# Moving the loads of the second expert matrices of teams two to seven from SyncE's DMA queue to ScalarE's

## What is computed

```python
a = jnp.einsum('nd,edf->nef', hf, w1)
b = jnp.einsum('nd,edf->nef', hf, w3)
y = jnp.einsum('nef,efd->nd', jax.nn.silu(a) * b * comb[..., None].astype(h.dtype), w2)
```

## Time and profile before

| | |
|---|---|
| median of 3 runs | 1349.12 us (1348.98 to 1349.36) |
| the profiled execution's own time | 1352.52 us |
| its span | 1350.7 us |
| mean granted clock of TensorE | 0.859 |
| busy share of the span: TensorE, VectorE, ScalarE | 73%, 24%, 23% |
| moved by DMA | 480.66 MB, mean 356 GB/s over the span |

### The profile page before, as it was taken

How to read it: one execution, slowest core, us unless ns; L and a number is a source line. 1 busy time by engine, 2 the same in 40 slices (tenths; PEclk the granted TensorE clock), 3 DMA queues, 4 the chain that set the end, 5 groups by cost and what they waited for, 6 DMA issues and landing times.

```text
span 1350.7 us, 18973 instructions
## 1 busy us (share of the span) xinstructions
PE 989.4 (73%) x8270; PEld 656.2 (49%) x8270; DVE 330.6 (24%) x504; ACT 307.1 (23%) x553; POOL 71.7 (5%) x48
## 2 busy tenths in 40 slices
PE   7999999999999974656576375647736664674647
PEld 6988887888888651333134133313413421341322
DVE  5557967544753200010010000001001000100101
ACT  6545555555542410001001000100100010010000
POOL 0000242500010020000000000000000000000000
PEclk9999999999999987678787777878868776886778
DMA  8745645544697999999999999999999999999997
GB/s 285 242 140 168 206 150 196 182 162 153 181 419 265 395 428 437 431 427 436 431 433 429 439 432 427 437 434 430 429 438 433 427 437 435 427 431 436 432 423 292
DMA packets 65458, 480.66 MB, mean 356 GB/s; under 512 B 7272, under 2 KB 11776, under 8 KB 48512
## 3 DMA queue, kind: packets, MB, share of 16 engines
q1 hardware_dynamic: 65408, 479.95, 86.7%
HBM read 477.84 MB, written 2.10 MB: 355 GB/s over the span
## 4 chain that ended last, share of the span: by engine, by line
DMA 48%; PE 47%; SPq 2%; DVE 1%; issue 1%; ACT 1%; DVEq 0%; ACTq 0%
DMA ring<-w_dram 47%; PE ps L1587 11%; PE ps L1330 9%; PE ps L1331 9%; PE ps L1332 9%; PE ps L1625 5%; SPq L487 1%; DVE w_split L879 1%; PE ps L1346 1%; DMA xs<-x_dram 1%; SPq L400 1%; PE ps L1542 1%; PE ps L1440 1%; PE ps L1362 0%; SPq L407 0%
## 5 line engine op out<-in xcount | busy, mean ns | idle before, releaser
L1587 PE MATMUL ps<-ring,side_buf 128*32 128x256 f32 x3968 | 273.4, 443 | 240.0 <-DMA ring<-w_dram 240.0
L1587 PEld LDWEIGHTS ps<-ring,side_buf 128*32 128x32 f32 x3968 | 155.7, 127 | 362.3 <-issue 309.2
L1330 PE MATMUL ps<-w_split,zT_half 128*128 128x512 f32 (+2 forms) x576 | 221.8, 385 | 1.8 <-DVE w_split L879 1.7
L1332 PE MATMUL ps<-w_split,zT_half 128*128 128x512 f32 (+2 forms) x576 | 218.6, 379 | 0.0
L1331 PE MATMUL ps<-w_split,zT_half 128*128 128x512 f32 (+2 forms) x576 | 218.5, 379 | 0.0
L879 DVE TENSOR_TENSOR w_split<-raw_buf,w_split 128x1024 fp32r<-128x1024 f32 (+2 forms) x144 | 182.0, 1282 | 147.2 <-ACT w_split L597 146.6
L1625 PE MATMUL ps<-ring,side_buf 128*32 128x512 f32 x960 | 129.4, 700 | 98.9 <-DMA ring<-w_dram 98.0
L597 ACT CAST w_split<-raw_buf 128x1024 fp32r<-128x1024 f32 (+2 forms) x144 | 143.5, 1016 | 113.9 <-PE ps L1332 108.9
L1256 DVE TENSOR_TENSOR xs<-xs,ps 128x512 f32<-128x512 f32 x56 | 38.5, 687 | 487.8 <-PE ps L1554 487.7
L817 ACT ACTIVATE side_buf<-ps,st 128x256 f32<-128x256 f32 x16 | 6.7, 471 | 545.2 <-PE ps L1587 545.2
L1625 PEld LDWEIGHTS ps<-ring,side_buf 128*32 128x32 f32 x960 | 38.0, 126 | 184.9 <-issue 184.9
(11 more groups left out here) (186 smaller groups left out, 493.2 us busy)
## 6 DMA issues: line engine op xcount, KB each, us to landing
ring<-w_dram SPq DMA_DIRECT2D x56, 4096.0 KB, 24.7
ring<-w_dram SPq DMA_DIRECT2D x72, 2048.0 KB, 21.3
raw_buf<-w_in_dram SPq DMA_DIRECT2D x47, 1024.0 KB, 5.0
raw_buf<-w_out_dram SPq DMA_DIRECT2D x16, 1024.0 KB, 5.8
spare<-w_dram SPq DMA_DIRECT2D x2, 2048.0 KB, 8.7
ring<-w_dram SPq DMA_DIRECT2D x4, 1024.0 KB, 12.1
ring<-w_dram SPq DMA_DIRECT2D x8, 512.0 KB, 11.4
raw_buf<-w_in_dram SPq DMA_DIRECT2D x4, 608.0 KB, 6.1
```

The costliest lines, as they stand in the source:

```text
L1330: mm(b, zhi(c)[:, t], wh, start=(c == 0), stop=False)
L1332: last = mm(b, zlo(c)[:, t], wh, start=False, stop=(c == C - 1))
L1587: last = mm(ps[part, up, pair * WIDE:(pair + 1) * WIDE], h_e[:, c, slots], w[m][:, cc * NB + h * WIDE:cc * NB + (h + 1) * WIDE], start=(c ...
```

## The change

SP's loop over teams one to six issues only the U groups. ScalarE's program issues D0 and D1 of these teams, on its own DMA queue, with the same waits on `ring_used`, the same sources, slots and semaphores. Each team's D0 loads stand ahead of the two silus, D1's behind them. Team 0 is taken out of ScalarE's loop, since SP loads it, and so is the last team.

```diff
             with sp.Fori(1, TEAMS - 1) as it:
-                team(it, it)
+                matrices(it, it)
...
-            def team(it):
+            def load_down(it, half):
+
+                for m in range(TEAM):
+                    k = UP_CHUNKS + TEAM * half + m
+                    act.wait_ge(ring_used, it * TEAM_CHUNKS + (k - RING + 1))
+                    act.dma_start(ring[:, chunk_slot(k), :],
+                                  w2_v[bass.ds(it * TEAM + m, 1), half].rearrange("o p n -> (o p) n")).then_inc(
+                                      landed[chunk_slot(k)], 16)
+
+            def team(it, loads=False):
+                if loads:
+                    load_down(it, 0)
                 activate(it)
+                if loads:
+                    load_down(it, 1)
                 gathered(it + 1)
                 turned(it)
                 act.wait_ge(ring_used, it * TEAM_CHUNKS + TEAM_CHUNKS)
...
-            with act.Fori(0, TEAMS - 1) as it:
-                team(it)
+            team(0)
+            with act.Fori(1, TEAMS - 1) as it:
+                team(it, loads=True)
```

## The result

The changed kernel takes 1371.12 us (median of 5 runs, 1364.86 to 1373.75), the one before 1349.36 in runs beside it: a ratio of 1.0156, 95% interval 1.0143 to 1.0169, 21.8 us slower. Forecast was no change. The measured time lies inside the stated range, near the number of rival A, but A is not what happened.

A forecast was written before the change was run, and what follows sets the result against it. The prediction took the kernel's expert stage as bound by DMA bytes at one steady rate. Moved issues, ScalarE's delays and queue sharing each cost 0 for six teams, leaving the median unchanged at 1349.1 us; range 1347 to 1374.

The forecast's parts named there:

- rival A: Queues share equal bytes: U3 lands late, stream empty before D1's rows, 3.95 us lost a team; 1372.8 us, chance 0.15.
- The bound: Expert stage, 573 to 1310 us: bytes divided by one steady rate, DMA share 1.00 at 432 GB/s, 116.4 us a team.
- Turns by row, two to one: Queues share by rows: U's are 32.7 KB, D's 16 KB, so U gets two thirds of the rate, D one third.
- U3 against D0: D0 competes with the landing U3, which lands at 840.15, 5.3 us late; margin at D1's issue 1.35 us, cost 0.
- D1 against the next U0: D1, 3.5 us left, gets one third beside U0, lands 6.9 us late; margin at next U1 1.15 us, cost 0.
- The start of a transfer: Time from a DMA's issue to its first rows: 1.5 us, with 0 and 2.5 also tried for D1's margin.
- ScalarE's delay of the gather: D1's four issues on ScalarE hold up the gather's first copies; gather, turns and D0's matmuls 1.2 us later, cost 0.
- The team that I took: The one team clocked before the change, U2's matmuls ending at 822.70, from which both margins were worked out.
- theory 1: Not in the prediction, made for the follow-up runs: turns by row, 3.4 us from issue to first row beside a busy queue.
- B: Small holes close the margins of about 1 us: 0.5 to 1.3 us a team, 1352 to 1357 us, chance 0.15.
- How long an issue takes on ScalarE: ScalarE's DMA issue time, shown by no row; at twice SP's time the delay would be 3.5 us, still inside.
- the prediction's estimate from its fastest group: Limit on any gain: every group at the fastest pace, 19.30 us, saves 0.55 us a team, 3.3 in six; 1345.8 at best.

The follow-up runs named there:

- experiment 3: Changed kernel plus three or six useless TensorE matmuls a team between the turns and D0's matmuls: 1353.13 us (1.0045) and 1352.4 us (1.0027).
- cut_rows: Changed kernel with each 4 MB load of U issued as two DMAs of 2 MB in 16 KB rows: 1360.21 us, 1.0088 to the kernel before.
- d0_on_act: Changed kernel with D1 given back to SP, only D0 on ScalarE's queue: 1350.6 us, 1.0005 to the kernel before.
- pad3: Changed kernel plus three useless TensorE matmuls between the turns and D0's matmuls of each team but the last: 1353.13 us, 1.0045 to the kernel before.
- act_warm: Changed kernel with one 8 KB load moved from SP's to ScalarE's queue at the start: 1367.51 us, 1.0130 to the kernel before.

## Why the prediction was wrong

**The bound: right.** The expert stage is bytes at one rate; in experiment 3 TensorE got more work and the time went down.

**Turns by row, two to one: right**, by the counts of rows (35 and 34) and by `cut_rows`. Two queues brought no bandwidth either, `d0_on_act` standing at 1.0005. The traces agree with the Trainium skill's rule that the prediction named ("DMA: Bandwidth & Descriptors", Rules for kernel authors): 431 GB/s there from 573 to 1310 us, and 432 before. The same page of the Trainium skill (Queues, rings and completion order) has an engine drain a whole packet, typically 9 to 17 descriptors, before it turns to the next queue. Here 16 engines moved 16 rows of one queue and then 16 of the other, one row a turn, and the measurement decides. Rival A's share of equal bytes does not occur with these rows. Its 1372.8 us is near the measured time by accident: the hole stands behind D1, not before it.

**U3 against D0: right in kind.** "lands at 840.15, 5.3 us late" was 3.4 in the team shown, and 4.2 where U2's matmuls take 7.11 us as in the earlier trace rows. A start 3.4 us after the issue, not 1.5, leaves U3 more time alone.

**D1 against the next U0: the step that failed.** The text had "The stream holds until 893.05: margin 1.15 us"; by the losses it was minus 1.5 to minus 3.8 in teams two to six, and minus 9.2 in team one. From U2's landing to D1's I had 65.2 us (815.45 to 880.65); it took 68.0 in the team shown (825.67 to 893.64) and 66.7 in one where U2's matmuls take 7.11 us (944.64 to 1011.37). And U1 landed 2.6 us later than its issue and 19.4 us of stream (903.30 to 925.32), where I had put 1.5; in the other teams it was 2.8 to 3.6. Term by term:

- *The start of a transfer.* "I put at 1.5 us", at most 2.5. It is 3.4 to 3.5 beside a busy queue. The bound came from the shortest landing in a trace in which no second queue ever came up beside a first.
- *ScalarE's delay of the gather.* "1.2 us later": D0's matmuls started 10.0 us after U3's (858.51 to 868.51), against 9.85 before, 0.15. Nor did D1's first issue wait for the silus: it began at 739.69, the second silu at 739.85. I counted both as costs that eat a margin. They would have protected the other one: `pad3` gives such a delay back.
- *The team that I took.* U2's matmuls take 7.11 us there, in other teams 8.80. The longer ones issue D0 later, so U3 is less late, so U0 is asked for sooner, with D1 4.6 and not 3.5 us from done; at a third of the rate each of these is paid three times.

With 3.4 us for every start and 0.15 us for the gather, the prediction's own sum gives a hole of about 0.9 us in a team where U2's matmuls take 7.11 us, and with U2's end 1.7 us later about 2.6 us. Recorded are 1.5 and 2.2 for the first kind, 2.5, 2.6 and 3.8 for the second. So these terms make most of the loss of teams two to six; up to 1.3 us a team stays open.

**The error behind these** is that I checked each margin for lateness alone. With two queues, being early does harm: by theory 1, one us less before the next U0 lets D1's rest grow by one and its landing by two. A margin of 1.15 us with a gear of two or three on terms known to 1 us is not "0"; the chance of 0.15 for B, small holes of 0.5 to 1.3 us, was too low and their size too small. B's kind of thing is what happened.

**Team one, 9.2 us: missed.** "How long an issue takes on ScalarE no row shows; at twice SP's time the delay would be 3.5 us" was right for 44 issues (344 ns) and wrong for the first four (4.97, 2.25, 0.93 and 1.34 us in the trace). By `act_warm` this is 3.6 us of the whole by the medians, 4.9 by team one's length; the remainder of the 9.2 is a hole at the same place as in the other teams. Why it is that large even with a warm queue was not tried. Theory 1 falls short here: 7 us left at 631, taken three times, land D1 near 652, and it landed at 656.46. By the packets D1 had only 2.02 MB left at 631, 4.7 us of stream, but its rows were spread out to the end (15 of 88 packets from 646 to 652). That would fit engines out of step, with the landing set by the last of them; it is argued from the counts, not shown.

The changed kernel's runs spread over 9 us, those of before beside it over 1.7. That would fit a hole that depends on fractions of a microsecond times three; only one run of each kernel has a trace, so it is not shown.

## What to carry to other kernels

On a saturated stream the order of service is a resource. Splitting it over two queues adds no rate, but lets a transfer that is wanted later take row-sized turns from one that is wanted now, in the ratio of the rows' lengths; keep what is used in order in one queue, or let the later one be issued only when the earlier is nearly in (on the third of four chunks here, not on the second or the fourth). Look for the instant at which nothing is queued, and ask of every delay whether it shields another transfer: here 2.2 us a team of useless work on TensorE were worth 18 us in all. No version of this case beat the kernel before, and by the prediction's estimate from its fastest group (435 GB/s, against 432) none of this kind could by more than about 3 us.

## What the runs showed of the hardware

- Two queues of one core take turns row by row on each of the 16 engines: 35 rows of 32 KB beside 34 of 16 KB in 4 us, and a chunk of 4.85 us in 14.5. With rows of 16 KB in both, 1.77 and 1.69 MB in 8 us.
- A transfer issued on an idle queue beside a busy one moves its first row about 3.4 us after the issue (issued 834.89, first rows between 838.0 and 838.5; 756.68, between 760 and 761). From an empty stream the first rows came sooner (issued 903.30, 13 rows between 904.0 and 904.5), but the next ones only from 906.0, and the group landed 2.6 us later than its issue and its 19.4 us of stream.
- The first DMA issues on ScalarE took 4.97, 2.25, 0.93 and 1.34 us, the later ones about 0.34; an 8 KB transfer on that queue at the start takes this away.
- A DMA issue on ScalarE begins while an ACTIVATE ahead of it still runs (739.69 beside 739.47 to 739.94).
- U's loads in rows of 16 KB instead of 32 KB, and twice as many transfers, in one queue: a team 116.7 us instead of 116.35, the kernel 1.0030.
